# Eight subtractions of shifted value rows move from VectorE to GpSimd, in a one-core encoder layer

## The reference

```python
proj = hn @ w_in
u, q, k, v = jnp.split(proj, ...)                 # 512 columns each, 8 heads of 64
z = einsum('bqhd,bkhd->bhqk', qi, k) * scale
log_beta, log_1m = log_sigmoid(z), where(valid, log_sigmoid(-z), 0)
suffix = cumsum(log_1m, reverse=True) - log_1m    # over keys
a = where(valid, exp(log_beta + suffix), 0)
attn = einsum('bhqk,bkhd->bqhd', a, v)
mix = concatenate([pool_out, attn]) @ w_out
```

## Time and profile before

| what | value |
|---|---|
| median of three runs | 804.96 us |
| profiled execution, its own time | 804.16 us |
| its span, first to last instruction | 802.4 us |
| granted TensorE clock, mean | 0.979 |
| DVE busy, 250 to 300 us | 44.95 of 50 us |
| PE busy, 250 to 300 us | 47.25 of 50 us |
| POOL busy, 250 to 300 us | 7.45 of 50 us |

### The profile page before, as it was taken

The page is one execution under the profiler, slowest core; times in us unless marked ns, Lnnn a source line. Parts: engine busy times, 40 slices in busy tenths (PEclk is TensorE's granted clock), DMA queues, the critical chain, the costliest instruction groups (busy, mean ns, idle before and its releaser), DMA issues. The chain is left out here.

```text
span 802.4 us, 13449 instructions
## 1 busy us (share of the span) xinstructions
PE 767.7 (96%) x4808; PEld 606.4 (76%) x4809; DVE 562.9 (70%) x621; ACT 374.6 (47%) x706; POOL 309.9 (39%) x261
## 2 busy tenths in 40 slices
PE   7999999999989899999999997799999999999995
PEld 4889999999975566767767786488888888888641
DVE  5759957762125995876787867998656999574178
ACT  4571212212246983554464528544444444544254
POOL 2100799990010300100000110367565899564156
PEclk9999999999999999999999996899999999999997
DMA  8947644715049701320202249967779998889695
GB/s 320 388 153 257 210 158 133 228 53 185 1 149 327 236 2 53 106 80 27 80 27 79 80 158 333 338 249 262 259 269 361 415 376 270 294 315 364 238 372 200
DMA packets 78442, 168.59 MB, mean 210 GB/s; under 512 B 6974, under 2 KB 32126, under 8 KB 76219
## 3 DMA queue, kind: packets, MB, share of 16 engines
q1 hardware_dynamic: 69154, 134.36, 47.9%
q0 software_dynamic: 8048, 29.36, 9.9%
q10 hardware_dynamic: 1192, 4.21, 1.5%
HBM read 132.57 MB, written 33.12 MB: 207 GB/s over the span
## 5 line engine op out<-in xcount | busy, mean ns | idle before, releaser
L2501 PE MATMUL psum<-we_hi,x_parts 128*128 x384 | 136.5, 402 | 0.8 <-ACT x_parts L2257 0.8
L2045 DVE TENSOR_TENSOR we_lo<-we_raw,we_hi 128x2048 fp32r<-128x2048 f32 x48 | 118.0, 2461 | 1.5
L490 PE MATMUL psum<-hn_hi,w_hi 128*128 128x364 f32 (+1 forms) x380 | 91.2, 332 | 1.3 <-DVE hn_lo L716 1.3
L490 PE MATMUL psum<-hn_lo,w_hi 128*128 128x364 f32 (+1 forms) x380 | 90.3, 329 | 0.0
L490 PE MATMUL psum<-hn_hi,w_lo 128*128 128x364 f32 (+1 forms) x380 | 90.0, 328 | 0.0
L2044 DVE CAST we_hi<-we_raw 128x2048 fp32r<-128x2048 f32 x44 | 59.6, 1355 | 39.5 <-DMA we_raw<-in_w_up_dram 25.6
L1279 PE MATMUL psum<-wo_hi,mixin 128*128 128x512 f32 (+1 forms) x256 | 82.9, 395 | 1.6 <-DVE logits L1646 1.1
L2501 PEld LDWEIGHTS psum<-we_hi,x_parts 128*128 128x128 f32 x384 | 72.1, 188 | 15.3 <-issue 1.1
L2501 PE MATMUL psum<-we_lo,x_parts 128*128 x192 | 75.4, 393 | 0.0
L793 DVE SCALAR_TENSOR_TENSOR proj<-early,cT,proj 128x2048 f32<-128x2048 f32 x28 | 72.1, 2616 | 1.5 <-DMA early<-in_w_mod_dram 1.3
L490 PEld LDWEIGHTS psum<-hn_hi,w_hi 128*128 128x128 f32 x380 | 66.6, 189 | 4.7 <-issue 2.3
(11 more groups left out here) (376 smaller groups left out, 1569.2 us busy)
## 6 DMA issues: line engine op xcount, KB each, us to landing
we_raw<-in_w_up_dram SPq DMA_DIRECT2D x32, 1024.0 KB, 8.4
early<-in_w_mod_dram SPq DMA_DIRECT2D x16, 1024.0 KB, 5.4
we_raw<-in_w_down_dram SPq DMA_DIRECT2D x16, 1024.0 KB, 7.0
w_raw<-in_w_in_dram SPq DMA_DIRECT2D x16, 512.0 KB, 6.2
we_raw<-ff_d SPq DMA_DIRECT2D x12, 512.0 KB, 7.2
proj<-in_x_prompt_dram SPq DMA_DIRECT2D x4, 1024.0 KB, 8.0
sc_room<-in_w_mod_dram SPq DMA_DIRECT2D x4, 1024.0 KB, 11.0
wo_raw<-in_w_out_dram SPq DMA_DIRECT2D x2, 2048.0 KB, 9.4
```

What stands on the lines that cost most here:

```text
L490: mm = pe.matmul(psum[:, 2 * c + slot, 0:n], w[:, slot, k, :], hn[:, k, t0:t0 + n], start=(k == 0 and w is w_hi and hn is hn_hi), stop=(k ...
L2045: dve.tensor_tensor(we_lo[:, a:b], raw, we_hi[:, a:b].bitcast(F32), ALU.subtract).then_inc(ready, 1)
L2501: mm = pe.matmul(psum[:, bank, :], x[:, s, k, :], w[:, bass.ds(at + k * 2 * DE, 2 * DE)], start=(k == 0 and x is x_hi and w is we_hi), sto ...
```

## The change

The eight prompt tiles' subtractions leave DVE's program and stand in POOL's, between the last memset of `block_b` and the wait for `rows_in`; the sample's stays on DVE. POOL first waits for the sample's count on `dv_ready`, so that the counts keep their order. The three transfers that bring the shifted rows are as before. In DVE_BESIDE the steps wl:0 to wl:7 stood at u = 15, 16, 18, 19, 20, 21, 23, 25 and stand at u = 14, 15, 16, 17, 18, 20, 22, 24.

```diff
 DVE_BESIDE = {
-    1: "DV:0", 7: "DV:1", 8: "DV:2", 9: "DV:3", 10: "DV:4", 11: "DV:5", 12: "DV:6", 13: "DV:7", 14: "DV:8", 15: "wl:0", 16: "wl:1", 18: "wl:2", 19: "wl:3", 20: "wl:4", 21: "wl:5", 23: "wl:6", 25: "wl:7", 26: "Pl:0", 28: "C0:0",
+    1: "DV:0", 14: "wl:0", 15: "wl:1", 16: "wl:2", 17: "wl:3", 18: "wl:4", 20: "wl:5", 22: "wl:6", 24: "wl:7", 26: "Pl:0", 28: "C0:0",
...
             pool.memset(logits[:, PT, :], 0.0).then_inc(b_const, 1)
+            pool.wait_ge(dv_ready, 1)
+            for n in range(1, TILES):
+                j = ORDER[n]
+                pool.wait_ge(before_in[group_of(n)], 16 * 3)
+                pool.tensor_tensor(dv[0:P, j, :], dv[0:P, j, :], v_st[0:P, j, :], ALU.subtract).then_inc(dv_ready, 1)
+
             pool.wait_ge(rows_in, 16 * 5)
...
-            def differences(n):
-
-                j = ORDER[n]
-                r, g = rows(j), group_of(n)
-                dve.wait_ge(before_in[g], 16 * (2 if g == 0 else 3))
-                dve.tensor_tensor(dv[0:r, j, :], dv[0:r, j, :], v_st[0:r, j, :], ALU.subtract).then_inc(dv_ready, 1)
+            def sample_differences():
+                dve.wait_ge(before_in[0], 16 * 2)
+                dve.tensor_tensor(dv[0:DEC, PT, :], dv[0:DEC, PT, :], v_st[0:DEC, PT, :], ALU.subtract).then_inc(dv_ready, 1)
...
                     if step == "DV":
-                        differences(n)
+                        sample_differences()
```

## The result

| | kernel before | changed kernel |
|---|---|---|
| median of nine runs | 806.26 us (803.69 to 807.83) | 811.02 us (806.63 to 813.18) |
| profiled execution, its own time | 804.16 us | 806.63 us |
| its span | 802.4 us | 804.9 us |
| mean granted clock, profiled execution | 0.979 | 0.977 |

The ratio is 1.0057, interval 1.0033 to 1.0080: slower by 4.6 us (2.7 to 6.4). The forecast was 807.6 with a range up to 810.6, that is +2.6 us (at most +5.6) on the median of 804.96 that it started from. The direction was right, but the measured time lies above the range. In part that is the base: the kernel before has a median 1.3 us higher in these runs than in the three that the forecast started from. The difference of the medians, 4.8 us, lies nearer the forecast's upper end than its centre.

A forecast was written before the change was run, and what follows sets the result against it. PE's program order was taken as the bound: 0 for DVE's relief, +2.6 us for turns between POOL and DVE, 0 for wl steps and POOL's tail, on the 804.96 us median, gave 807.6 us, range 804.0 to 810.6.

The forecast's parts named there:

- What bounds the stretch: Between 254 and 296 us PE's program order is the path; DVE is full but in time, so relieving it gains 0.
- GpSimd's duration: Each 128x512 subtraction on POOL takes 1.27 us undisturbed, read from a line between two other sizes.
- The hold: Time each POOL subtraction keeps a DVE scan waiting: 1.05 us, with ends of 0.8 and 1.27.
- They take turns: POOL and DVE two-input operations on SBUF each wait for the other's running instruction, so subtractions and scans of units 9 to 12 alternate.
- Unit 12's lateness: Unit 12's scans ready at 266.36 us where PE wants them at 262.66: 3.7 us late.
- The walk's last step: After unit 12 PE regains 1.1 us where it used to idle for ACT, leaving a lasting shift of +2.6 us.
- later units run on two free engines at their old speed: After the subtractions end, units behind unit 12 lose nothing more, so the +2.6 us shift stays to the end.
- rival 1: Full price: every subtraction holds DVE for its whole 1.27 us and scans hold POOL; +4.4 us, 809.4; chance 0.25.
- rival 2: Scans don't block with POOL, or PE's margins swallow it: +0, 805.0 us; chance 0.23.
- rival 3: DVE's fullness from 265 to 290 us is the real limit, so 5.3 us less work gives at most 799.7; chance 0.10.
- POOL's tail: What queues behind or waits for POOL's subtractions (values(8), wh:2, zero DMAs, iotas) stays within its margins: 0.
- the wl steps: Eight 1.20 us DVE steps moved one or two units sooner: worth 0, tightest at unit 18; without cover 1.2 us once.

The follow-up runs named there:

- e4: Changed kernel with GpSimd writing constants to the eight difference tiles, subtraction left out; whole time not comparable, unit 8 to 26 in 41.8 us as before.
- e9: Kernel before with VectorE's eight subtractions in later places (two each in units 9 and 10, one each in 11 to 14); 807.78 us, ratio 1.0008.
- e1: Changed kernel with 11 spare matmuls on PE filling its waits before turn(11) and turn(12); 807.04 us, ratio 1.0013 to the kernel before.
- e2: Changed kernel without the moved wl steps, only the subtractions on GpSimd; 811.18 us, ratio 1.0043 to the kernel before.
- e3: Kernel before, subtractions still on VectorE, with only the wl steps moved to the change's units; 808.37 us, ratio 1.0009.
- e8: Changed kernel with GpSimd scaling the tiles in place, one input, instead of subtracting; routing differs, unit 8 to 26 shifted 0.0 us against the kernel before.
- e5: Kernel before, GpSimd idle, with five spare VectorE operations making the scans of units 11 and 12 late; 808.81 us, ratio 1.0036.
- e6: Kernel before with five spare VectorE operations making scans late, and 11 spare matmuls filling PE's waits; 807.24 us, ratio 1.0014.
- e10: Kernel before with VectorE's subtractions later and ScalarE's copy_att ahead of its high-part copies; 804.96 us, ratio 0.9981.

## Why the prediction was wrong

- *What bounds the stretch*: right. PE's order is the path, DVE's fullness is not. In e4, 5.3 us less work on DVE bought nothing in the stage, and e9 removed the DMA stall for nothing.
- *GpSimd's duration*: 1.27 forecast, 1.28 for the first, which began before a scan was beside it. Right.
- *The hold*: 1.05 forecast, 1.02 to 1.03 measured. Right, as was that a scan is subject to it. "They take turns" was only half right: GpSimd's step grew from 1.28 to 1.38 us only (1.65 for the last, which had 256-column scans beside it). Nearly the whole loss is VectorE's, and the forecast had that in its sum by letting POOL's start-up lie under the scan.
- *Unit 12's lateness*: 3.7 us forecast; turn(12) came at 265.96 - 0.21 (the later start of that execution) against 262.66, 3.1 late.
- *The walk's last step failed*: "PE catches up only where it used to idle", -1.1 us, and the +2.6 that was to remain. In the changed kernel PE caught up nothing: 3.09 us late at turn(12), 3.09 late at unit 26. The idle pieces did go (2.5 to 1.2 us of waiting for ACT), but PE, idle for 1.07 and 1.86 us, came back to a clock at its lower level, and the same work took 1.23 us more up to unit 16. From unit 14's scores to unit 15's the shift grows from 1.15 to 2.62 us, mostly by the second wait, and by unit 16's it is 3.05, where the catching up should have lowered it. Nor is the clock the whole of it. With the clock held, in e1, PE was 2.70 us late at turn(12) and 2.29 at unit 26: it caught up 0.4 and not 1.1, as units 13, 17 and 18 had late scans too, which "later units run on two free engines at their old speed" left out. In e2, with the longer fall, it went from 2.79 to 3.90. So against e1 the clock adds 0.4 us in the changed kernel's profile and 1.5 in e2's. The missing terms are this clock, whose size differs from one execution to the next, and the scans that stayed late. That the stage's +3.1 lies near +2.6 comes of a lateness forecast 0.6 too large and a catching up forecast 1.1 too large.
- *The rivals*: rival 1 gave 809.4 by a full hold of 1.27 us. The total came out near it and its mechanism did not: the hold is 1.03. Rivals 2 and 3 fell, rival 2 by the scans' durations, rival 3 by PE's waits and by e4, where an emptier VectorE gained nothing.
- *POOL's tail and the wl steps*: POOL's last subtraction ended at 265.35 and wh:2 began at 272.08 without waiting for it; the zero DMAs began as before. For the low parts see e3; in e1 PE did wait for the scans of units 17 and 18, behind wl steps that had moved, and no run tells whether these steps or the lateness before them was the cause.

Open: the medians differ by 4.8 us, the profiled stage by 3.1 (3.9 in e2), and the changed kernel's profiled execution, its fastest, is 0.8 us nearer the kernel before at its end than at unit 26. e2's profiled execution is 7.0 us longer in span, 3.1 of them behind unit 26. A longer fall of the clock in other executions would fit, and means of the granted clock point that way (0.9744 over nine runs after and 0.9720 in e2, against 0.9773 in e1 and 0.9777 over 26 of the kernel before), but those have no profile. The interval, 2.7 to 6.4 us, holds the stage's figure too.

## What to carry to other kernels

When an operation moves to an idle engine, look at how many inputs it reads from SBUF and what runs beside it. A 1.28 us subtraction with two inputs on GpSimd put 1.03 us on each scan beside it, where doing it on VectorE had cost 0.67; a one-input operation put 0.2 to 0.4 us on some. When a step makes PE wait in a dense stretch, add to the wait what the clock may take afterwards, and test it by filling the wait with spare matmuls. Don't count old idle time as slack for catching up until the engine that was late is on time again. Look at which engine releases PE before relieving a busy one: here ScalarE's order gave 1.0 us in the stage for three lines.

## What the runs showed of the hardware

- One input or two: beside GpSimd's two-input subtraction every scan took 1.02 to 1.03 us more. Beside e8's one-input operation four of thirteen instructions took 0.20 to 0.43 us more, those that began in its first half microsecond. Beside e4's writes none did. The Trainium skill (SBUF — State Buffer, Who interferes with whom) has a VectorE instruction with two SBUF inputs contend with a GpSimd instruction that reads SBUF, and not with one that only writes it. The trace agrees with both halves. It differs on how long: by the rule that the prediction drew on, the second waits until the first has finished, but a scan that began 0.27 us into a scaling of 1.49 us was held for 0.20 us only. The measurement decides. Beside another VectorE instruction a small one-input copy on GpSimd did wait, 2.13 us.
- Waits of PE and the clock: in the three profiles with PE's waits for late scans left open (changed kernel, e2, e5; the longest 1.1 to 1.9 us) the lower clock followed for 3 to 7 us. In the two with the waits filled (e1, e6) it did not. Of the nine others two show a fall between 264 and 272 us with no wait over 0.7 us (e3, e9), and in e6 a wait of 2.28 us before 258.43 was followed by none. So the waits make the fall likely here and do not decide it. It also fell near 240 us in four of the profiles (e3, e4, e5, e10), whatever had been changed.
- The same three transfers of shifted rows landed between 254.0 and 257.0 us.
